# Gate projections as seven half-block products instead of eight in a two-block transformer kernel

## The reference, cut to what matters

```python
# first block, per layer (x is already normed)
f = (jax.nn.silu(x @ w_gate[l]) * (x @ w_up[l])) @ w_down[l]
# second block, twice per layer
def swiglu(x, w_gate, w_up, w_down):
    return (jax.nn.silu(x @ w_gate) * (x @ w_up)) @ w_down
h = x + 0.5 * swiglu(rms_norm(x, ffn1_norm[l]), ffn1_gate[l], ffn1_up[l], ffn1_down[l])
```

## Time and profile before

| | value |
|---|---|
| median of 3 runs | 3143.73 us (3143.63 to 3143.93) |
| span of the profiled execution | 3141.2 us |
| PE busy, PEld busy | 3116.4, 2588.2 us |
| DVE, ACT, POOL busy | 1147.4, 713.8, 2259.0 us |
| mean granted TensorE clock | 0.998 |

### The profile page before, as it was taken

How to read it: one execution, slowest core, us unless ns; L and a number is a source line. 1 busy time by engine, 2 the same in 40 slices (tenths; PEclk the granted TensorE clock), 3 DMA queues, 4 the chain that set the end, 5 groups by cost and what they waited for, 6 DMA issues and landing times.

```text
span 3141.2 us, 44673 instructions
## 1 busy us (share of the span) xinstructions
PE 3116.4 (99%) x15518; PEld 2588.2 (82%) x15518; DVE 1147.4 (37%) x1874; ACT 713.8 (23%) x1474; POOL 2259.0 (72%) x3079
## 2 busy tenths in 40 slices
PE   8999999999999999999999999999999999999999
PEld 7879888898798888888887788888888887788887
DVE  5575111275751112632226542212222136542211
ACT  4453110054531100411112321110211022321100
POOL 5347877673468776788777398887888777398884
PEclk9999999999999999999999999999999999999999
DMA  5112322231123222232232132223222232132222
GB/s 185 48 41 86 109 93 95 93 108 42 47 88 104 96 95 90 84 102 98 95 112 92 41 101 95 98 95 100 94 94 100 94 111 88 41 108 94 100 94 68
DMA packets 83017, 284.07 MB, mean 90 GB/s; under 512 B 9531, under 2 KB 15068, under 8 KB 82652
## 3 DMA queue, kind: packets, MB, share of 16 engines
q1 hardware_dynamic: 77484, 273.70, 26.2%
q10 hardware_dynamic: 5424, 8.79, 0.8%
HBM read 278.79 MB, written 3.67 MB: 90 GB/s over the span
## 4 chain that ended last, share of the span: by engine, by line
PE 97%; DVE 2%; ACT 1%; issue 0%; DMA 0%; DVEq 0%; ACTq 0%
PE bank_v L537 21%; PE bank_v L539 20%; PE bank_v L538 20%; PE bank_a L537 9%; PE bank_a L539 9%; PE bank_a L538 9%; PE bank_v L881 1%; PE bank_a L860 1%; PE bank_s L1021 1%; PE bank_s L899 1%; PE bank_v L1036 1%; PE bank_s L591 0%; PE bank_s L1024 0%; PE bank_a L584 0%; PE bank_s L889 0%; PE bank_s L907 0%
## 5 line engine op out<-in xcount | busy, mean ns | idle before, releaser
L511 POOL TENSOR_TENSOR w_lo<-raw,w_hi 128x512 fp32r<-128x512 f32 x1024 | 1414.7, 1382 | 81.8
L508 POOL TENSOR_TENSOR zero<-zero 128x1 f32<-128x1 f32 x1024 | 277.3, 271 | 769.0 <-PE bank_v L539 578.8
L537 PE MATMUL bank_v<-xn_hi,w_hi 128*128 128x512 f32 (+1 forms) x1680 | 640.9, 381 | 8.1 <-DVE xn_lo L1700 8.0
L509 POOL CAST w_hi<-raw 128x512 fp32r<-128x512 f32 x1024 | 639.1, 624 | 0.0
L539 PE MATMUL bank_v<-xn_hi,w_lo 128*128 128x512 f32 (+1 forms) x1680 | 635.0, 378 | 0.0
L538 PE MATMUL bank_v<-xn_lo,w_hi 128*128 128x512 f32 (+1 forms) x1680 | 634.6, 378 | 0.0
L537 PE MATMUL bank_a<-xn_hi,w_hi 128*128 128x512 f32 (+1 forms) x1232 | 469.0, 381 | 2.3 <-ACT work L1248 1.4
L539 PE MATMUL bank_a<-xn_hi,w_lo 128*128 128x512 f32 (+1 forms) x1232 | 466.7, 379 | 0.0
L538 PE MATMUL bank_a<-xn_lo,w_hi 128*128 128x512 f32 (+1 forms) x1232 | 466.6, 379 | 0.0
L537 PE MATMUL bank_v<-h_hi,w_hi 128*128 128x512 f32 (+1 forms) x1122 | 422.9, 377 | 0.0
L538 PE MATMUL bank_v<-h_lo,w_hi 128*128 128x512 f32 (+1 forms) x1122 | 422.4, 376 | 0.0
(11 more groups left out here) (357 smaller groups left out, 3114.5 us busy)
## 6 DMA issues: line engine op xcount, KB each, us to landing
raw<-in_w_stream SPq DMA_DIRECT2D x516, 512.0 KB, 3.3
rope<-in_rope ACTq DMA_DIRECT2D x2, 1024.0 KB, 5.7
da_v<-t_rows ACTq DMA_DIRECT2D x2, 1024.0 KB, 6.5
out<-resid SPq DMA_DIRECT2D x8, 256.0 KB, 2.3
t_rows<-t_row ACTq DMA_DIRECT2D x1, 1536.0 KB, 7.4
resid<-in_x ACTq DMA_DIRECT2D x5, 256.0 KB, 7.2
mla_v<-in_alibi ACTq DMA_DIRECT2D x2, 512.0 KB, 7.5
resid<-in_x SPq DMA_DIRECT2D x3, 256.0 KB, 9.4
```

Source lines behind the costliest of these rows:

```text
L508: pool.tensor_tensor(zero[:, 1:2], zero[:, 0:1], zero[:, 0:1], ALU.add)
L509: pool.tensor_copy(w_hi[:, u, cut], raw[:, u, cut]).then_inc(*hi_split.done(("unit", u, n)))
L511: ins = pool.tensor_tensor(w_lo[:, u, cut], raw[:, u, cut], w_hi[:, u, cut].bitcast(F32), ALU.subtract)
L537: pe.matmul(out, lhs_hi, rhs_hi, start=first, stop=False)
```

## The change

Within each network the gate projections of tiles 4 to 21 are made in nine pairs (`PLAIN` = 4, `PAIRED` = 9). For a pair, the two weight units a and b and the tokens form 2x2 block matrices: w11, w12 are the first and second 512 columns of a (chunks 0 to 3 and 4 to 7), w21, w22 those of b; x11, x12, x21, x22 are the activations of chunks 0 to 3 and 4 to 7, tokens 0 to 255 and 256 to 511. Strassen's scheme in Winograd's form makes the 2x2 product from seven block products in place of eight. Each is 4 chunks by 3 matmuls of 256 tokens, so a pair takes 84 matmuls of 256 tokens where it took 48 of 512. Up projections and tiles 0 to 3 stay as they were. The weight stream is reordered: gate, gate, up, up for a pair.

- Token sums t (four of 128x4x256 each) are formed and split once per network by DVE (sums, lo) and ACT (hi), after tile 1. In FFN-B they are formed from `scaled_x`, eight new 128x512 ACT copies of `resid` times the norm's gain.
- Weight sums S1 to S4 are formed for each pair by DVE and split by ACT and DVE, as is w22. POOL splits only unit a; for unit b it waits for DVE's lo of w22, issues one small addition and signals both units.
- Products go into half banks of `bank_s`; ACT and DVE combine them (u2, u3, c22, c21, c12), then Silu.
- The product of gate and up is stored as float32 `hidden`, in the place of `h_lo`. The sums t and S occupy the place of `h_hi` until the last pair, so all 22 tiles are split to hi and lo only after the last pair's last product (`hidden_hi`, `last_hidden`).
- SP's and POOL's loops over the stream are written out.

The core of the diff:

```diff
-            with loop(pool, "stream", UNITS // SLOTS - 1):
-                for u in range(SLOTS):
-                    pool.wait_ge(*raw_in[u].after("unit"))
...
+            for n in range(SLOTS, UNITS):
+                u = n % SLOTS
+                if n - 1 in GATE_UNITS:
+                    pool.wait_ge(weights_lo.sem, len(LO_PARTS) * GATE_UNITS[n - 1] + RAW_FREE)
+                    pool.tensor_tensor(zero[:, 2:3], zero[:, 0:1], zero[:, 0:1], ALU.add).then_inc(w_split.sem, 2)
+                    continue
...
+            def gate_products(tag, at, j):
...
+                pe.wait_ge(*c11_read.before((tag, at, "c11")))
+                pe.wait_ge(*c12_read.before((tag, at, "c12")))
+                unit((tag, at, "gates"))
+                multiply(bank_11, w11, x11).then_inc(*multiplied.done((tag, at, "p1")))
+                split("S23")
+                multiply(bank_22, s2, t2).then_inc(*multiplied.done((tag, at, "p6")))
+                multiply(bank_21, s3, t3).then_inc(*multiplied.done((tag, at, "p7")))
+                split("S1")
+                multiply(bank_12, s1, t1).then_inc(*multiplied.done((tag, at, "p5")))
+                pe.wait_ge(*act_step.after((tag, at, "p1")))
+                multiply(bank_11, w12, x21, True).then_inc(*multiplied.done((tag, at, "p2")))
+                pe.wait_ge(*combined.after((tag, at, "u3")))
+                multiply(bank_21, w22, t4, True).then_inc(*multiplied.done((tag, at, "p4")))
+                split("S4")
+                pe.wait_ge(*combined.after((tag, at, "c22")))
+                multiply(bank_12, s4, x22, True, {0: half_used.done((tag, at, "gates"), 2), 1: w_used.done((tag, at, "gates"), 2)}
+                         ).then_inc(*multiplied.done((tag, at, "p3")))
```

DVE's part (ACT's mirrors it), in the order of its queue in FFN-B:

```diff
+            def last_hidden(tag, finish):
+                for f in range(FC):
+                    if f in (FC // 2 - 1, FC - 2):
+                        finish(f // (FC // 2))
+                    dve.wait_ge(*x_hi.after((tag, "h", f)))
+                    dve.tensor_tensor(h_lo[:, f, :], hidden[:, f, :], h_hi[:, f, :].bitcast(F32), ALU.subtract
+                                      ).then_inc(*x_lo.done((tag, "h", f)))
...
+                def pair(at, j):
+                    combine_early(tag, at)
+                    dve.wait_ge(*multiplied.after((tag, at, "p2")))
+                    dve.tensor_tensor(work[:, 0, HALVES[0]], bank_11, scale_by[:, HALVES[0]], ALU.mult
+                                      ).then_inc(*c11_read.done((tag, at, "c11")))
+                    dve.wait_ge(*combined.after((tag, at, "c22")))
+                    scale_part(1, 1, value.done((tag, at, "c22")))
+                    if at != "last":
+                        pair_sums(tag, at, j + 1)
+                    combine_21(tag, at)
+                    dve.wait_ge(*combined.after((tag, at, "c21")))
+                    scale_part(1, 0, value.done((tag, at, "c21")))
+                    combine_12(tag, at)
+                    dve.wait_ge(*c12_read.after((tag, at, "c12")))
+                    scale_part(0, 1, value.done((tag, at, "c12")))
+                    if at != "last":
+                        pair_lo(tag, at)
+
+                first(0, 0)
+                first(0, 1)
+                column = C2[tag]
+                dve.wait_ge(*act_step.after(("scaled_x", column, DC - 1)))
+                token_sums(tag, scaled_x)
+                first(1, 0)
+                first_pair(tag)
+                first(1, 1)
+                with loop(dve, tag, PAIRED - 1) as i:
+                    pair("pair", i)
                     for k in range(2):
...
+                        finish("pair", k, bass.ds(i * 2 + (PLAIN + k), 1))
+                pair("last", None)
+                last_hidden(tag, lambda k: finish("last", k, slice(FC - 2 + k, FC - 1 + k)))
```

More of the change, by code:

```diff
@@ L383, in build @@
         stat_bank = bank_s[3]
+        bank_11, bank_12, bank_21, bank_22 = (b[:, 0:HALF] for b in bank_s)
         out_in_scores = bank_s[1]
@@ new lines, in ffn_paired, with second_hidden @@
+            def ffn_paired(tag):
+                for n in range(4):
+                    pe.wait_ge(*x_lo.after((tag, "t", n)))
+                with loop(pe, tag, PAIRED - 1) as i:
+                    gate_products(tag, "pair", i)
+                    for k in range(2):
+                        project((tag, "pair", "up", k), v_bank)
+                gate_products(tag, "last", PAIRED - 1)
+                for k in range(2):
+                    project((tag, "last", "up", k), v_bank)
+            def second_hidden(tag):
+                for k in range(2):
+                    project((tag, "gate1", k), a_bank)
+                    project((tag, "up1", k), v_bank)
@@ L1347, in norm_ln @@
                 act.wait_ge(*affine.after((tag, DC - 1, 1)))
-            def ffn(tag):
[L1350 to L1362, removed]
@@ L1366, in leave_bank, with keep_scaled_x, ffn_scaled @@
+            def keep_scaled_x(column, c):
+                act.activation(scaled_x[:, c, :], resid[:, c, :], ACT.Copy, scale=par2[:, column + c:column + c + 1]
+                               ).then_inc(*act_step.done(("scaled_x", column, c)))
+            def ffn_scaled(tag, stats, kept=False):
                 def leave_bank(key):
@@ L1676, in _ @@
                 gained("rms3", C2["ffn2"], lambda c: act.wait_ge(*end_kept(c)))
+                for c in range(DC):
+                    keep_scaled_x(C2["ffn2"], c)
+                act.wait_ge(*act_step.after(("scaled_x", C2["ffn2"], DC - 1)))
                 act.wait_ge(*x_lo.after(("rms3", DC - 1)))
@@ L1683, in _ @@
                     gained("next", C2["ffn1"], lambda c: act.wait_ge(*v_read.after(("ffn2", "down", c))))
+                    with counts.within("layer2", l + 1):
+                        for c in range(DC):
+                            keep_scaled_x(C2["ffn1"], c)
                 else:
@@ L1941, in ffn_scaled @@
                     for k in range(2):
-                        hidden(k, slice(2 * n + k, 2 * n + k + 1), f"gate{n}", f"up{n}", f"h{n}")
-                with loop(dve, tag, FC // 2 - done) as i:
-                    for k in range(2):
-                        hidden(k, bass.ds(i * 2 + (2 * done + k), 1), "gate", "up", "h")
+                        finish("pair", k, bass.ds(i * 2 + (PLAIN + k), 1))
+                pair("last", None)
+                last_hidden(tag, lambda k: finish("last", k, slice(FC - 2 + k, FC - 1 + k)))
@@ L2460, in _ffn_units @@
     out = []
-    for g, u in zip(_proj_units(gate), _proj_units(up)):
-        out += [g, u]
+    gates, ups = _proj_units(gate), _proj_units(up)
+    for f in range(PLAIN):
+        out += [gates[f], ups[f]]
+    for f in range(PLAIN, FC, 2):
+        out += [gates[f], gates[f + 1], ups[f], ups[f + 1]]
     tiles = down.reshape(FC, P, DC, P).transpose(1, 2, 0, 3).reshape(P, FC, UNIT)
```

351 lines of the change are left out of this document (282 added, 69 removed).

## The result

The changed kernel takes 3163.98 us (median of 4 runs, 3163.3 to 3164.4), the kernel before 3143.72 beside it: 1.0065 of before, interval 1.0051 to 1.0079. It is 20.3 us slower where 13.3 were forecast. Spans: 3162.6 against 3141.2 us, 21.4 more.

What follows compares the result with a forecast made beforehand. PE was taken to bound the kernel, busy for 3116.4 of 3141.2 us. 3141.2 - 43.7 (pairs) + 29.0 (ends) + 14.8 (FFN-A starts) + 13.2 (first FFN-B) gave a 3154.5 us span, 3157.0 on the median; range 3127 to 3180.

Steps and rivals of the forecast that it cites:

- the likeliest case: Whole kernel: gain and waits come out as forecast, 3148 to 3172 us; chance 0.52.
- the gain: Pairs' gates on PE: 84 matmuls take 10.07 us instead of 10.88, saving 43.7 us over 9 pairs and 6 networks.
- the ends: Behind each network's last pair PE waits for late splits: 5.9 us per FFN-B, 2.7 per FFN-A, 29.0 in all.
- the first FFN-B: Before its first pair PE waits 11.2 us behind DVE's queue after the late factor; 13.2 in all, bounds 10 to 18.
- the other FFN-B: Start of the three later FFN-B: DVE's chain just meets PE's 21.76 us, so 0, bound above 3 each.
- FFN-A's starts: POOL's units come late beside DVE's token sums: PE waits 7.4 us in each of two, 14.8 in all.
- rival 2: In the pairs the 256-token step is 113.3 ns, half of 226.7, so the gain is 73.4 us: 3127 us; chance 0.07.
- The loop: Rounds inside the FFN loops lose nothing, with a margin of about 2.5 us; bounds 0 to 1 us a round.
- rival 3: The loop itself binds in FFN-B if a turn is 1.3 us, 1 us x 32 rounds: 3189 us; chance 0.10.
- The turns: DVE's two-SBUF operations alternate with busy POOL: 1.1 us each instead of 0.60; operations with one PSUM input aren't stretched.
- Rival 1: DVE passes at 0.60 us beside POOL, so network ends and FFN-A starts cost nothing: 3112 us; chance 0.10.
- Rival 4: Waits and gain cancel: FFN-A starts 6, ends 24, first FFN-B 13, so 3143 us, give or take 8; chance 0.18.

Runs made afterwards that it cites:

- experiment 2: Changed kernel with the 22 `h_lo` subtractions at each network's end reading a PSUM bank in place of `h_hi` (values wrong): 3131.76 us, ratio 0.9963.
- Experiment 1: Changed kernel with the two `finish` calls at a network's end moved before subtractions 4 and 10, in place of 10 and 20: 3156.39 us, ratio 1.0041.
- experiment 3: Changed kernel with the second operand of the eight 128x1024 token-sum instructions read from PSUM (values wrong): 3149.53 us, ratio 1.0016.
- Experiments 4 and 5: Changed kernel, first FFN-B: token and first pair's sums queued ahead of tiles 0 and 1, 3162.19 us; then token sums moved ahead of the factor's copy, 3161.23 us.
- experiment 5: Changed kernel; in the first FFN-B token sums made before DVE copies the factor, first pair's weight sums directly behind, ahead of the tiles: 3161.23 us, ratio 1.0057.
- experiment 6: The kernel of experiment 5 with the factor multiplies of the first FFN-B's first four tiles cut to 2 of 512 columns (values wrong): 3155.55 us, ratio 1.0040.
- the fastest kernel: Changed kernel with splits as places come free, first FFN-B's sums ahead of the factor, FFN-A's token sums ahead of the first two tiles: 3128.01 us, ratio 0.9951.

## Why the prediction came out as it did

The time lies in the likeliest case, 3148 to 3172, but the forecast was 8.1 us of span too low. Four terms miss that way: the gain by 1.6, the ends by 4.3, the first FFN-B by 1.6, the other FFN-B by 2.4. One misses the other way, FFN-A's starts by 1.6.

**The gain** was right in its mechanism: 84 matmuls took 10.07 us, as worked out. The step of 119.9 ns, read where PEld was busy for 4.00 of 4.00 us, held for the products, and rival 2 falls. The round took 20.98 us for 20.95, which is 1.6 us over the 54 rounds: 42.1 gained for 43.7.

**The loop** had no wait, and rival 3 falls. The margin was put at 2.5 us and is larger: four extra instructions, 4.75 us of DVE a round, cost nothing. The unrolled loops of SP and POOL, for which nothing was charged, cost nothing that shows: the other terms make up the span to 0.2 us.

**The end of a network** is where the forecast was most too low: 29.0 against 33.3. The mechanism and its pace were right, as the first up matmul behind p3 and the last subtractions of the second FFN-B show:

```profile
2082.29 0.40 PE L588 MATMUL bank_v<-xn_hi,w_hi 128*128 128x512 f32 x1
...
2110.86 2.38 DVE L2173 TENSOR_TENSOR h_lo<-hidden,h_hi 128x512 fp32r<-128x512 f32 x2
```

The last one ended 31.0 us after p3 (2113.24 for 2082.29), where 31.1 was worked out. From one subtraction to the next it was 1.11 us in the mean, in steps of 0.60, 1.0 and 1.7; experiment 2 takes the term away. Two things were mis-sized. In FFN-A the wait of 2.3 us came near the forecast (2.7), and then a stretch at half clock, which the sum had left out, added 1.7 in chunk 0. In FFN-B the first wait is for the bank (4.1 us), a step that was worked out for FFN-A only; with it PE stands once and long instead of 22 times and short, and a stretch at half clock follows: 6.0 to 6.6 against 5.9. Experiment 1, which has no long gap, measures 5.7 for FFN-B. So of the 4.3 us too little, 2.7 are FFN-A's (3.5 of clock less 0.8 of wait) and 1.6 are FFN-B's.

**The turns.** The stretch on both sides, read from the earlier trace rows, is there again at the end of the changed kernel's networks and gone in experiment 2 (a half unit of POOL 3.33 and 2.07 us). That an operation with one input in PSUM isn't stretched was said without a row. Experiment 2 shows it for `h_lo`, 678 ns in the mean against 1218, and in the changed kernel the two multiplies of `bank_v` (L1956) at the end of the second FFN-B take 678 ns among the stretched subtractions.

**The start of FFN-A** was forecast at 14.8 and took 13.2, and is this close partly by luck. The wait of 3.8 us came, at 310.78. One of 0.7 came a unit earlier, at 301.32; of those of 1.9 and 1.7 for the later units no more than 0.3 came, and 1.7 of halved clock, which was not in the sum, did. That the turns cause it is shown by experiment 3 (14.4 us gone). The changed kernel's POOL rows in experiment 3 have its addition at 1.19 us beside DVE's sum of 1.22 (296.22 to 297.44). The prediction took a turn of 1.1 for an instruction of 1024 columns; the eight start 1.1 to 2.2 us apart and take 12.2 us together, 1.52 each.

**The first FFN-B** was forecast at 13.2, 11.2 of it wait and 2 clock, and took 14.8 (13.4 and 1.4). The 2 us for the clock was the author's estimate, and no run of the kernel before shows the term: of its three stretches at a granted 0.50, those from 36.6 and 900.2 us (3.4 us each) have no gap over 0.6 us from start to start in the 9 us ahead of them, and the last one, from 3136 us on, has no PE work in it. In the changed kernel the granted clock is 0.50 from 1320.7, inside the pause, to 1334.2, so for 3.0 us behind it, and costs 1.4. The wait's cause was put down to DVE's queue behind the late factor. Experiments 4 and 5 show that another order isn't enough. In experiment 5, with the sums first, DVE works 36.1 us from its first sum to the end of u3 (1296.91 to 1332.99), and PE has work for 26 of them: the pauses of 1.75 and 8.29 us are the rest. Less work for DVE shortens it: in experiment 6 the longer pause fell from 8.3 to 3.9 us.

**The other FFN-B** have 1.2 us in two of three, where the forecast said that DVE's chain "just meets" its time. In experiment 3 they have none, so it was the turns again.

**The rivals.** Rival 1 (the turns don't bind) falls with the step of 1.11 us. Rival 4 had all three of its terms too small: 6 for the starts of FFN-A against 13.2, 24 for the ends against 33.3, 13 for the first FFN-B against 14.8. What stood in the last 0.03 of the chances, the clock halved at the ends of networks too, came at all six ends of the profiled execution, and the time stayed under 3172 all the same.

What stays open: why FFN-A's gap of 2.5 us before the down projection is followed by the lower clock in some executions and not in others (behind 9 of 16 such gaps, as listed below). No run tried it by itself.

## What to carry to other kernels

A saving on the engine that bounds the kernel is paid for in the engines beside it, and mostly at the ends of the loop: here the loop had 6.4 us of room a round and lost nothing, while the starts and ends of the networks, without that room, cost 63.7 us against 42.1 gained. Work that is put off "until the places are free" should be begun place by place, behind the last reader of each; that alone turned a loss of 0.65% into no loss, and with two changes of order at the starts into a gain of 0.5%. And where DVE and POOL run side by side, count DVE's two-SBUF instructions by turns (here 1.11 us from one of 128x512 to the next, for 0.60 with POOL waiting), and expect a long one to delay each POOL instruction next to it by most of its length (here by 0.84 to 1.00 of 1.2 us).

## What the runs showed of the hardware that was not expected

The lower clock after short gaps. The window (as above: busy times, then the granted clock) at the start of the first FFN-A's down projection, behind a gap of 2.5 us, and that of the pause in the first FFN-B:

```profile
515.00:518.40 3.40, 3.40 (x10) 2.63 (x9) 3.40 (x4) 0.26 (x1) 3.32 (x4) 0.50 0.02 5
...
1321.00:1334.00 13.00, 2.82 (x13) 2.82 (x14) 12.70 (x17) 5.14 (x9) 3.83 (x4) 0.50 0.14 47
```

In the first, eight matmuls start in 3.4 us, 0.43 us apart where they are 0.23 apart at a granted 1.00. All of it is busy, at a granted 0.50. The stretch costs 1.7 us, two thirds of the gap before it. Gaps are given here from start to start, from one trace of each kernel that kept these ends. Behind each of the 28 gaps of 4.3 us at the start of an FFN-B's down projection such a stretch came (3.4 or 6.8 us long), behind the 16 gaps of 2.5 us in FFN-A in 9 cases. In the kernel with eight extra multiplies the FFN-B gaps are 3.0 us, with a stretch behind 2 of 4, and behind 10 of the 21 gaps of 2.4 to 2.5 us before p1 in its loop. Behind the 12 gaps of 1.0 to 2.1 us in the three kernels that split as the places come free there was none.

A gap's length alone doesn't decide it. In 6 of the 14 traces a stretch also begins near 1290 to 1297 us, where PE stands for 1.3 and 1.2 us within 5 us, and in the other 8 none does. In the fastest kernel two stretches are left, beside that of its last microseconds. So a gap of 4.35 us costs 6.0 to 6.6, and the same lateness spread over 22 gaps costs 5.7.

Four full instructions of DVE in each of these rounds, where it was busy for 14.57 of 21 us, had no effect; eight cost 2.3% of the time.
